# One triangular inverse per level for two directions in an RWKV-7 recurrence, on one Trainium2 core

## The chip, the core and the metric

One Trainium2 chip, one core of it. The metric is the device time of one execution of the whole program, in microseconds, the median of the runs. TensorE (PE in the profile) does the matrix products and reads its moving operand and its weights from SBUF; VectorE (DVE), ScalarE (ACT) and GpSimd (POOL) do the elementwise work; SyncE (SP) issues the DMAs. Everything here is fp32.

## What is computed

Two layers of a hybrid backbone block over 256 context and 512 latent tokens of width 1024. Layer 0 mixes tokens with a bidirectional RWKV-7, layer 1 with grouped-query attention; a SwiGLU feed-forward follows each. The change is in the scan of layer 0, which runs once forward (e = 0) and once backward (e = 1) for each of 16 heads of 64 channels:

```python
def step(S, inp):
    r_t, w_t, k_t, v_t, kk_t, a_t = inp
    sa = jnp.einsum('bhvk,bhk->bhv', S, -kk_t)
    S = (S * w_t[:, :, None, :] + sa[..., None] * (kk_t * a_t)[:, :, None, :]
         + v_t[..., None] * k_t[:, :, None, :])
    return S, jnp.einsum('bhvk,bhk->bhv', S, r_t)
...
for d, rev in enumerate((False, True)):
    S_c, yc_d = rwkv7_scan(S0, r_c, d_c[d], k_c[d], v_c, kk_c, a_c[d], rev)
    _, yl_d = rwkv7_scan(S_c, r_l, d_l[d], k_l[d], v_l, kk_l, a_l[d], rev)
```

## The kernel before

The function `recurrence` (L909) cuts the 768 tokens into 12 chunks of 64 (`CH`) and processes a chunk at a time. Within a chunk the influence of earlier tokens on later ones is a 64x64 triangular system, so for each chunk, head and direction the inverse of a unit triangular matrix is needed. The forward matrix is triangular in one sense, the backward one in the other. Two heads are worked on together (a pair, 8 in all): partitions 0 to 63 hold one head, 64 to 127 the other (`half(h)`). A group is 4 chunks in each direction (`GROUP` = 4), 3 groups a pair, 24 groups in all; each of the tiles `inverse`, `inverse_t`, `lvl` holds 8 matrices of 64 columns, the forward ones in columns 0 to 255, the backward ones in 256 to 511.

The work of a group:

- `score` (PE, L1506 and L1509) and `mask` (DVE, L1778): the score matrices, cut to their triangles, into `sc_b` and `sc_k`.
- The inverse by doubling, in levels n = 0 to 5: at level n the inverse of blocks of 2^n is grown to blocks of 2^(n+1). `cut` (POOL, L2037) multiplies the scores by the mask of the level into `lvl`, 512 columns. `level0` (DVE, L1784) adds the identity. For n = 1 to 5: `t` (PE, L1549) multiplies `lvl` with the transposed inverse so far, 16 products of 64x64; `t_copy` (ACT, L1927) brings them to SBUF as `t_sb`, 512 columns; `y` (PE, L1559 and L1562) multiplies by the inverse so far, 16 products; `add` (DVE, L1790) adds the new blocks, 256 columns; `flip` (DVE, L1799) makes the transpose for the next level. The products of the backward direction have their heads crossed, so `swap` (ACT, L1939) copies the backward half of the inverse with the heads exchanged into `inverse_swapped`, two copies of 64x256 a level.
- The chain over chunks, 4 steps a group, 96 in all: `rhs` (PE, L1620), `rhs_copy` (ACT, L1944), `u` (PE, L1649, with the inverse as weights), `u_copy` (ACT, L1948), `products` (PE, L1664 and others), `update` (DVE, L1809) and `decay` (POOL, L2026).

Beside that run the features of the next pair and the readout of an earlier one (`feature`), on all engines.

The order is written out by hand: `period` is a long list of calls such as `t(at(-5), 3)`, run for each pair, and each engine's class takes from this one list the calls that are its own, in this order. Nothing is reordered afterwards, so an engine whose next instruction waits holds up everything behind it. Two PSUM work areas of two banks (`WORK`) are handed out in turn to `score`, `keys`, `values`, `t`, `y` and side work; `work_free` waits until the previous user of the area has been read.

A product of 64x64 takes a quarter of PE's array: the rows by the half of the partitions that its operands are read from, the columns by the half that its result goes to. In the profile one fp32 product is two MATMUL and two LDWEIGHTS records, so the 16 products of a `t` are 32 MATMUL records.

`values` (PE, L1536) has products in two quarters alone: rows of head h, columns of head 1 - h. The masks are loaded at the start (L1459, L1461).

Of the kernel before, what the change touches and what calls it, by code (L numbers as in the profile page):

```python
# [908 lines left out]
def recurrence(c, d, dram, hidden, full):  # L909

    nc = c.nc
    with ExitStack() as ctx:
# [41 lines left out]
        lvl_ready, t_ready, t_copied, x_ready, x_added, x_turned, x_swapped = (sem(n) for n in (  # L954
            "level_masked", "t_product", "t_copied", "x_products", "x_added", "x_turned", "x_swapped"))
# [13 lines left out]
        by_way = lambda bank: bank[:].rearrange("p (e n) -> p e n", e=2)[:, :, 0:GROUP * CH]  # L969
        def new_columns(units, way, n):  # L970

            size = 1 << n
            return bass.AP(units.tensor, units.offset + size,
                           [units.ap[0], [way - size, 2], [2 * size, GROUP * CH // (2 * size)], [1, size]])

        tokens_of = lambda bank: bank[:, 1024 - TOK:1024]
# [36 lines left out]
        def schedule(E):  # L1013
# [71 lines left out]
            def swap(G, n):  # L1085
                if G:
                    use.take("swap", G.g, n)
                    E.swap(G, n)

# [45 lines left out]
            def period(pair):  # L1135
# [13 lines left out]
                swap(at(-5), 1)  # L1149
# [26 lines left out]
                swap(at(-5), 2)  # L1176
# [16 lines left out]
                swap(at(-5), 3)  # L1193
# [13 lines left out]
                swap(at(-4), 0)  # L1207
# [16 lines left out]
                swap(at(-5), 4)  # L1224
# [9 lines left out]
                swap(at(-4), 1)  # L1234
# [24 lines left out]
                swap(at(-4), 2)  # L1259
# [27 lines left out]
                swap(at(-4), 3)  # L1287
# [5 lines left out]
                swap(at(-3), 0)  # L1293
# [17 lines left out]
                swap(at(-4), 4)  # L1311
# [5 lines left out]
                swap(at(-3), 1)  # L1317
# [25 lines left out]
                swap(at(-3), 2)  # L1343
# [29 lines left out]
                swap(at(-3), 3)  # L1373
# [13 lines left out]
                swap(at(-2), 0)  # L1387
# [19 lines left out]
                swap(at(-3), 4)  # L1407
# [3 lines left out]

            for name in FIRST:
                feature(0, name)
# [12 lines left out]
        with nc.Block() as block:  # L1426
# [338 lines left out]
            def _(dve):  # L1765
                v = nc.vector

                class Dve(Part):

                    def mask(self, G, i):  # L1770
                        dve.wait_ge(scores, self.use.of("score", G.g, i) + 1)
                        need(dve, y_ready, GROUP * (G.g - 3) + 2 * i + 2)
                        if G.g == 0:
                            dve.wait_ge(masks_loaded, 48)
# [1682 lines left out]
```

## Time and profile before

| | us |
|---|---|
| median of 3 runs (2299.14 to 2301.2) | 2301.01 |
| the profiled execution's own time | 2302.0 |
| its span | 2300.2 |
| PE busy | 2042.9 (89%) |
| PE weight loads busy | 1770.0 (77%) |
| DVE busy | 1248.9 (54%) |
| ACT busy | 931.0 (40%) |
| POOL busy | 491.1 (21%) |

The span is from the first to the last instruction of the program; 1.8 us lie around it. A busy share is a union over an engine's records: a MATMUL record of 64 columns lasts some 0.22 us, but the next starts long before it ends, so a busy PE may well be waiting. How fast PE works is read from the starts of its records, not from its busy share. The recurrence's matrices are worked on from about 402 us to 988 us of the span.

### The profile page before, as it was taken

Reading aid. Unit: us, or ns where it says so; the run is one execution under the profiler, and the core shown is the slowest. Engines: PE = TensorE matmul, PEld = TensorE weight load, DVE = VectorE, ACT = ScalarE, POOL = GpSimd, SP = SyncE. Lnnn points to the kernel's source line nnn. Section 1 sums busy time; section 2 is a strip of 40 time slices with the busy share of each in tenths; the row PEclk is TensorE's granted clock in tenths of the full one; section 3 lists DMA queues with packets and bytes.
Section 4 is the critical chain, followed back from the end, with each engine's and each line's share of the span. In section 5 each row is a group of like instructions: output and inputs, shape, how many; then the busy total and the mean of one; then the engine's idle time right before and its main releaser. Section 6 shows DMA issues by size and latency. Waiting matters only on the chain. (4 is left out here: it accounts for less than half of the span.)

```text
span 2300.2 us, 60266 instructions
## 1 busy us (share of the span) xinstructions
PE 2042.9 (89%) x26295; PEld 1770.0 (77%) x26295; DVE 1248.9 (54%) x1816; ACT 931.0 (40%) x1567; POOL 491.1 (21%) x410
## 2 busy tenths in 40 slices
PE   5798997788888887769999999999997988999998
PEld 3597886677767766669999999999863567888887
DVE  4544424677766775332885766755496534333333
ACT  2323324667666664422632322423334533432321
POOL 0011111776667765302000000001220001000000
PEclk8899998999999999979999999999898998999999
DMA  9676764000011000042121212211210012333332
GB/s 315 206 214 199 215 196 132 27 24 20 28 33 34 23 14 12 11 164 63 37 92 58 90 56 74 69 60 39 74 46 19 1 52 67 100 101 91 93 107 84
DMA packets 222295, 192.07 MB, mean 83 GB/s; under 512 B 11482, under 2 KB 206948, under 8 KB 221540
## 3 DMA queue, kind: packets, MB, share of 16 engines
q1 hardware_dynamic: 222052, 188.44, 26.7%
q8 instruction: 199, 3.26, 0.6%
q14 instruction: 44, 0.36, 0.1%
HBM read 170.60 MB, written 17.83 MB: 82 GB/s over the span
## 5 line engine op out<-in xcount | busy, mean ns | idle before, releaser
L2037 POOL TENSOR_TENSOR lvl<-sc_b,level_mask 128x512 f32<-128x512 f32 x144 | 204.6, 1432 | 90.3 <-PE banks L1549 53.6
L530 DVE TENSOR_TENSOR ffn_lo<-ffn_raw,ffn_hi 128x1024 fp32r<-128x1024 f32 (+1 forms) x58 | 77.5, 1335 | 195.3 <-ACT ffn_hi L525 195.3
L550 PE MATMUL banks<-mix_hi,proj_hi 128*128 128x386 f32 (+1 forms) x432 | 152.6, 353 | 14.2 <-DVE proj_lo L530 14.2
L550 PE MATMUL banks<-operand_hi,ffn_w_hi 128*128 128x384 f32 x464 | 156.3, 337 | 4.4 <-DVE operand_lo L496 4.4
L550 PE MATMUL banks<-operand_lo,ffn_w_hi 128*128 128x384 f32 x464 | 156.1, 336 | 0.0
L550 PE MATMUL banks<-operand_hi,ffn_w_lo 128*128 128x384 f32 x464 | 155.9, 336 | 0.0
L420 POOL TENSOR_TENSOR norm_squares<-norm_squares,norm_x 128x768 f32<-128x768 f32 (+1 forms) x18 | 29.8, 1657 | 588.1 <-ACT norm_x L414 588.1
L550 PE MATMUL banks<-mix_lo,proj_hi 128*128 128x386 f32 (+1 forms) x432 | 147.8, 342 | 0.0
L550 PE MATMUL banks<-mix_hi,proj_lo 128*128 128x386 f32 (+1 forms) x432 | 147.6, 342 | 0.0
L550 PE MATMUL banks<-operand_hi,ffn_hi 128*128 128x512 f32 x352 | 138.4, 393 | 5.2 <-DVE operand_lo L496 2.8
L525 ACT CAST ffn_hi<-ffn_raw 128x1024 fp32r<-128x1024 f32 (+1 forms) x60 | 68.3, 1139 | 182.7 <-PE banks L550 182.4
L550 PE MATMUL banks<-operand_hi,ffn_lo 128*128 128x512 f32 x352 | 137.9, 392 | 0.0
L550 PE MATMUL banks<-operand_lo,ffn_hi 128*128 128x512 f32 x352 | 137.9, 392 | 0.0
L2804 ACT CAST ffn_w_hi<-ffn_raw 128x512 fp32r<-128x512 f32 (+1 forms) x116 | 68.8, 605 | 131.7 <-PE banks L550 131.1
L868 POOL TENSOR_TENSOR mix_lo<-mix_full,mix_hi 128x769 fp32r<-128x769 f32 x24 | 40.6, 1692 | 318.0 <-ACT mix_hi L835 318.0
L1549 PE MATMUL banks<-inverse_t,lvl 64*64 64x64 f32 x3840 | 89.6, 225 | 20.4 <-issue 17.2
L550 PE MATMUL banks<-ffn_t_hi,ffn_w_hi 128*128 128x384 f32 x320 | 106.9, 334 | 0.0
L550 PE MATMUL banks<-ffn_t_lo,ffn_w_hi 128*128 128x384 f32 x320 | 106.9, 334 | 0.0
L550 PE MATMUL banks<-ffn_t_hi,ffn_w_lo 128*128 128x384 f32 x320 | 106.9, 334 | 0.0
L550 PEld LDWEIGHTS banks<-mix_hi,proj_hi 128*128 128x128 f32 x432 | 82.6, 191 | 29.7 <-DVE proj_lo L530 14.4
L1939 ACT COPY inverse_swapped<-inverse 64x256 f32<-64x256 f32 x240 | 96.8, 403 | 11.4 <-DVE inverse L1790 6.9
L2971 DVE SCALAR_TENSOR_TENSOR residual_stream<-banks,mod,residual_stream 128x256 f32<-128x256 f32 x144 | 60.8, 477 | 73.4 <-PE banks L550 73.2
(308 smaller groups left out, 6002.0 us busy)
## 6 DMA issues: line engine op xcount, KB each, us to landing
mod_raw<-in_mod_w SPq DMA_DIRECT2D x96, 512.0 KB, 6.1
ffn_raw<-in_ff_w SPq DMA_DIRECT2D x32, 1024.0 KB, 5.3
ffn_raw<-in_ff_w SPq DMA_DIRECT2D x46, 512.0 KB, 3.8
ffn_raw<-in_ff_w SPq DMA_DIRECT2D x16, 704.0 KB, 4.5
proj_raw<-in_rw_wr SPq DMA_DIRECT2D x8, 512.0 KB, 4.5
proj_raw<-in_rw_wk SPq DMA_DIRECT2D x8, 512.0 KB, 4.7
proj_raw<-in_rw_wv SPq DMA_DIRECT2D x8, 512.0 KB, 4.6
rwkv_out_raw<-in_rw_wo SPq DMA_DIRECT2D x8, 512.0 KB, 4.1
```

The lines of the kernel that those rows point to most:

```text
L420: pool.tensor_tensor(self.pool_sum[:, self.at0:], self.pool_sum[:, self.at0:], self.x[:, s, self.at0:], ALU.add)\
L525: signal(act, self.nc.scalar.copy(self.hi[s][:, 0:k_tiles, :], self.raw[s][:, 0:k_tiles, :]), self.rounded, self.at + n + 1)
L530: signal(eng, eng.tensor_tensor(self.lo[s][:, 0:k_tiles, :], self.raw[s][:, 0:k_tiles, :], self.hi[s][:, 0:k_tiles, :].bitcast(F32), ALU.s ...
L550: mm = pe.matmul(out, a, b, start=(first and n == 0), stop=(last and n == 2), skip_group_check=onto)
L868: signal(pool, nc.gpsimd.tensor_tensor(column(mix_lo[q % 2], k), full[s][:], column(mix_hi[q % 2], k).bitcast(F32), ALU.subtract), mix_res ...
L1549: mm = pe.matmul(bank[half(h ^ e), out], lvl[G.parity][n % 2][half(h), w, :], inv_t[G.parity][half(h), w, :], start=True, stop=True)
L1939: ins = a.copy(inv_s[G.parity][half(1 - h)], inv[G.third][half(h), GROUP:2 * GROUP, :])
L2037: g.tensor_tensor(lvl[G.parity][n % 2][:].rearrange("p (e q) t -> p e q t", e=2), sc_b[G.third][:, :, :, 0, :].rearrange("p q e t -> p e q ...
L2804: nc.scalar.copy(w_hi[x.n % SLOTS][:, 0:x.k_tiles, :], source(x)).then_inc(rounded, 1)
L2971: v.scalar_tensor_tensor(h[:, m, at:at + width], c.bank[bank_no(self, "down", part, m, q)][:, col:col + width], c.mod[:, 0, 40 + m, r:r + ...
```

## The change

The forward and the backward correction of a level lie in different blocks of a 64x64 matrix (the one above, the other below the diagonal). The change puts both in one matrix. `t` takes the lower block of one direction and the upper of the other from one `lvl` matrix of 256 columns in all, and reads the inverses of both directions as its moving operand, alternately 2^n columns of one and of the other (`kept_blocks`). `y` likewise (`new_blocks`), and its result lies in PSUM as two runs of columns, as do the scores. `t` and `y` have 8 products each where there were 16, all of them from head h's rows to head h's columns. `t_copy` moves 256 columns where there were 512. `swap`, its tile and its semaphore are gone, from PE's wait too. `cut` has 256 columns for n = 1 to 5, gathered from both directions' scores in runs of 2^n; for n = 0 it is two instructions of 256. The score tiles have another order of dimensions, so that this gathering is one pattern. The masks of both directions are loaded by 8 DMAs where there were 3, the level masks into a tile that is free then (`tok2`), and joined by one POOL instruction over 1536 columns (`join_masks`). The list of calls is the same but for the 15 `swap` calls taken out.

```diff
-        level_mask, score_mask = sb("level_mask", [P, LEVELS, 2, CH]), sb("score_mask", [P, 2, 2, CH])
+        level_mask, score_mask = sb("level_mask", [P, LEVELS, GROUP, CH]), sb("score_mask", [P, 2, 2, 2, CH])
-        sc_b, sc_k = ([sb(f"sc_{n}{s}", [P, GROUP, 2, 2, CH]) for s in range(3)] for n in "bk")
+        sc_b, sc_k = ([sb(f"sc_{n}{s}", [P, 2, 2, GROUP, CH]) for s in range(3)] for n in "bk")
-        inv_s = [sb(f"inverse_swapped{s}", [P, GROUP, CH]) for s in range(2)]
-        t_sb = [sb(f"t_sb{s}", [P, 2 * GROUP, CH]) for s in range(2)]
-        lvl = [[sb(f"lvl{s}{n}", [P, 2 * GROUP, CH]) for n in range(2)] for s in range(2)]
+        t_sb = [sb(f"t_sb{s}", [P, GROUP, CH]) for s in range(2)]
+        lvl = [[sb(f"lvl{s}{n}", [P, (2 - n) * GROUP, CH]) for n in range(2)] for s in range(2)]
...
+        def kept_blocks(units, n, count):
+            size = 1 << n
+            return bass.AP(units.tensor, units.offset, [units.ap[0], [2 * size, count * CH // (2 * size)], [way_units + size, 2], [1, size]])
+        def new_blocks(units, n, count):
+            size = 1 << n
+            return bass.AP(units.tensor, units.offset + size, [units.ap[0], [way_units - size, 2], [2 * size, count * CH // (2 * size)], [1, size]])
+        def lower_blocks(scores, n):
+            size, way = 1 << n, 2 * GROUP * CH
+            return bass.AP(scores.tensor, scores.offset, [scores.ap[0], [2 * size, GROUP * CH // (2 * size)], [way + size, 2], [1, size]])
+        by_way = lambda bank, n: bank[:, 0:GROUP * CH].rearrange("p (b a x) -> p b a x", b=2, x=1 << n)
...
                     def t(self, G, n):
...
                         for q in range(GROUP):
-                            for e in range(2):
-                                w, out = GROUP * e + q, slice(512 * e + q * CH, 512 * e + q * CH + CH)
-                                for h in range(2):
-                                    mm = pe.matmul(bank[half(h ^ e), out], lvl[G.parity][n % 2][half(h), w, :],
-                                                   inv_t[G.parity][half(h), w, :], start=True, stop=True)
+                            for h in range(2):
+                                out = bank[half(h), q * CH:q * CH + CH].rearrange("p (a b x) -> p a b x", b=2, x=1 << n)
+                                mm = pe.matmul(out, lvl[G.parity][n % 2][half(h), q, :],
+                                               kept_blocks(inv_t[G.parity][half(h), q:q + 1, :], n, 1), start=True, stop=True)
...
                     def y(self, G, n):
...
-                        pe.wait_ge(x_swapped, self.use.of("swap", G.g, n - 1) + 1)
                         for q in range(GROUP):
                             for h in range(2):
-                                pe.matmul(bank[half(h), q * CH:q * CH + CH], t_sb[G.parity][half(h), q, :],
-                                          inv[G.third][half(h), q, :], start=True, stop=True)
-                            for h in range(2):
-                                mm = pe.matmul(bank[half(h), 512 + q * CH:512 + q * CH + CH],
-                                               t_sb[G.parity][half(1 - h), GROUP + q, :], inv_s[G.parity][half(1 - h), q, :],
-                                               start=True, stop=True)
+                                out = by_way(bank, n)[half(h), :, q * (CH // 2 >> n):(q + 1) * (CH // 2 >> n), :]
+                                mm = pe.matmul(out, t_sb[G.parity][half(h), q, :],
+                                               new_blocks(inv[G.third][half(h), q:q + 1, :], n, 1), start=True, stop=True)
...
-                        a.copy(t_sb[G.parity][:].rearrange("p (e q) t -> p e (q t)", e=2), by_way(work(self.use, "t", G.g, n)))\
-                            .then_inc(t_copied, 1)
-
-                    def swap(self, G, n):
...
-                        for h in range(2):
-                            ins = a.copy(inv_s[G.parity][half(1 - h)], inv[G.third][half(h), GROUP:2 * GROUP, :])
-                        ins.then_inc(x_swapped, 1)
+                        a.copy(flat(t_sb[G.parity][:]), work(self.use, "t", G.g, n)[:, 0:GROUP * CH]).then_inc(t_copied, 1)
...
+                    def join_masks(self):
+                        pool.wait_ge(masks_loaded, 128)
+                        ways = [tok[2][:, e, 0:LEVELS, :].unsqueeze(2).to_broadcast([P, LEVELS, GROUP, CH]) for e in range(2)]
+                        g.tensor_tensor(level_mask[:], ways[0], ways[1], ALU.add).then_inc(masks_joined, 1)
...
-                        g.tensor_tensor(lvl[G.parity][n % 2][:].rearrange("p (e q) t -> p e q t", e=2),
-                                        sc_b[G.third][:, :, :, 0, :].rearrange("p q e t -> p e q t"),
-                                        level_mask[:, n].unsqueeze(2).to_broadcast([P, 2, GROUP, CH]), ALU.mult)\
-                            .then_inc(lvl_ready, 1)
+                        if n == 0:
+                            for e in range(2):
+                                ins = g.tensor_tensor(lvl[G.parity][0][:, e * GROUP:(e + 1) * GROUP], sc_b[G.third][:, 1 - e, 0],
+                                                      level_mask[:, 0], ALU.mult)
+                        else:
+                            blocks = {"b": 2, "x": 1 << n}
+                            ins = g.tensor_tensor(flat(lvl[G.parity][n % 2][:, 0:GROUP]).rearrange("p (a b x) -> p a b x", **blocks),
+                                                  lower_blocks(sc_b[G.third][:], n),
+                                                  flat(level_mask[:, n]).rearrange("p (a b x) -> p a b x", **blocks), ALU.mult)
+                        ins.then_inc(lvl_ready, 1)
```

In the order of ACT's instructions, a stretch of the steady part of the recurrence before (copies `tok`, `t_sb`, `inverse_swapped`, `rhs`, `u_sb` and the side work of the features):

```order
401 L1948 COPY u_sb<-banks 128x128
402 L1915 COPY tok<-banks 128x1024
403 L1927 COPY t_sb<-banks 128x512
404 L1939 COPY inverse_swapped<-inverse 64x256 x2
405 L1927 COPY t_sb<-banks 128x512
406 L1944 COPY rhs<-banks 128x128
407 L1975 ACTIVATE ep<-cum 128x12x64
408 L1948 COPY u_sb<-banks 128x128
```

and the same place of another pair in the changed kernel (its lines have other numbers):

```order
415 L1907 COPY tok<-banks 128x1024
416 L1919 COPY t_sb<-banks 128x256 x2
417 L1923 COPY rhs<-banks 128x128
418 L1954 ACTIVATE ep<-cum 128x12x64
419 L1927 COPY u_sb<-banks 128x128
```

The copies of the swapped inverse are gone, those of `t_sb` have half the columns, and all else stands in its old order. On PE, near the recurrence's start, before:

```order
1470 L1549 MATMUL banks<-inverse_t,lvl 64x64 x32
1471 L1559 MATMUL banks<-inverse,t_sb 64x64 x2
1472 L1562 MATMUL banks<-inverse_swapped,t_sb 64x64 x2
...
1487 L1536 MATMUL banks<-centre_heads,v_pair 64x64 x16
1488 L1549 MATMUL banks<-inverse_t,lvl 64x64 x32
```

and now:

```order
1449 L1544 MATMUL banks<-inverse_t,lvl 64x64 x16
1450 L1554 MATMUL banks<-inverse,t_sb 64x2x32 x16
1451 L1532 MATMUL banks<-centre_heads,v_pair 64x64 x16
1452 L1544 MATMUL banks<-inverse_t,lvl 64x64 x16
```

Two `t` and two `y` one behind the other have 16 products each where they had 32, and the `values` products stand where they stood.

## Rows read from the trace of the kernel before

**Rows 1.** Busy time by stretch of the recurrence; the x is the number of records
```profile
core 0: us, PE busy (x) PEld busy (x) DVE busy (x) ACT busy (x) POOL busy (x), PEclk, DMA share, GB/s
480.00:900.00 420.00, 345.20 (x13087) 295.11 (x13088) 289.27 (x434) 269.34 (x545) 289.55 (x259) 0.98 0.09 26
sum 586.00, PE 474.64 PEld 404.34 DVE 375.88 ACT 356.89 POOL 376.91; mean PE 158.21 PEld 134.78 DVE 125.29 ACT 118.96 POOL 125.64
```
**Rows 2.** PE's waits from 402 to 988 us: total us, times, longest us
```profile
PE banks L1549 <- issue: 17.2, 17, 2.2
PE banks L1562 <- issue: 7.7, 8, 1.3
...
PE banks L1559 <- issue: 6.8, 8, 1.2
PE banks L1620 <- DVE state L1809: 6.0, 7, 1.3
PE banks L1664 <- ACT u_sb L1948: 5.7, 15, 0.5
...
PE banks L1689 <- issue: 0.6, 1, 0.6
```
**Rows 3.** Instruction queue, 402 to 988, then 480 to 900 us: packets, MB, share
```profile
q8 instruction: 141, 2.31, 1.6%
...
q8 instruction: 104, 1.70, 1.7%
```
**Rows 4.** PE in order of time: start us, us, what, records, idle before
```profile
502.76 0.27 PE L1593 MATMUL banks<-vtok,tok 64*64 64x64 f32 x2 [1.22 <-issue]
502.89 0.27 PE L1559 MATMUL banks<-inverse,t_sb 64*64 64x64 f32 x2
...
503.38 0.31 PE L1506 MATMUL banks<-ar,b 64*64 64x128 f32 x2
...
556.21 0.63 PE L1536 MATMUL banks<-centre_heads,v_pair 64*64 64x64 f32 x15
556.71 0.27 PE L1559 MATMUL banks<-inverse,t_sb 64*64 64x64 f32 x2
```
**Rows 5.** Groups by line and shape, ACT and POOL: busy us, mean ns, idle before
```profile
L1939 ACT COPY inverse_swapped<-inverse 64x256 f32<-64x256 f32 x240 | 96.8, 403 | 11.4 <-DVE inverse L1790 6.9
L1927 ACT COPY t_sb<-banks 128x512 f32<-128x512 f32 x120 | 70.1, 585 | 55.1 <-PE banks L1549 55.1
L1921 ACT COPY vtok<-banks 128x256 f32<-128x256 f32 x8 | 3.0, 373 | 7.2 <-PE banks L1536 7.2
L2037 POOL TENSOR_TENSOR lvl<-sc_b,level_mask 128x512 f32<-128x512 f32 x144 | 204.6, 1432 | 90.3 <-PE banks L1549 53.6 <-DVE sc_b L1778 31.7 <-DVE inverse L1784 5.0
L2015 POOL TENSOR_TENSOR diag<-ident_heads,ends 128x256 f32<-128x256 f32 x44 | 26.9, 630 | 0.0
```
**Rows 6.** POOL, then DVE, in order of time at the recurrence's start
```profile
386.53 3.04 POOL L2015 TENSOR_TENSOR diag<-ident_heads,ends 128x256 f32<-128x256 f32 x4 [27.48 <-DVE ends L1874]
403.38 2.48 POOL L2037 TENSOR_TENSOR lvl<-sc_b,level_mask 128x512 f32<-128x512 f32 x2 [13.81 <-DVE sc_b L1778]
...
397.70 0.69 DVE L1778 TENSOR_TENSOR sc_b<-banks,score_mask 128x512 f32<-128x512 f32 x1 [1.24 <-PE banks L1509]
```
**Rows 7.** SP's DMA issues at the start, and the level masks' time to landing
```profile
375.16 1.29 SPq L1461 DMA_DIRECT2D level_mask<-in_k_level_mask  x2
376.49 1.44 SPq L1463 DMA_DIRECT2D lora_w<-in_rw_w  x1
...
DMA to landing us min/median/max: 5.5/5.9/6.2
```
**Rows 8.** Stretches of 3.4 us, columns as in Rows 1
```profile
719.70:723.10 3.40, 2.66 (x52) 2.58 (x55) 1.96 (x3) 1.22 (x2) 1.05 (x3) 1.00 0.20 63
723.10:726.50 3.40, 3.40 (x134) 3.40 (x132) 1.91 (x4) 1.75 (x5) 2.06 (x2) 0.51 0.26 77
...
791.40:794.80 3.40, 2.47 (x57) 2.26 (x49) 3.00 (x6) 2.02 (x3) 0.92 (x3) 1.00 0.23 63
794.80:798.20 3.40, 3.40 (x95) 3.38 (x99) 0.51 (x2) 1.83 (x5) 0.86 (x1) 0.50 0.23 58
...
941.60:945.00 3.40, 1.45 (x92) 1.31 (x84) 2.08 (x3) 1.18 (x2) 2.98 (x4) 1.00 0.02 5
945.00:948.40 3.40, 3.07 (x80) 2.76 (x73) 1.03 (x3) 1.66 (x4) 1.63 (x2) 0.50 0.02 5
```

More of the change, by code:

```diff
@@ L1083, in flip @@
                     E.flip(G, n)
[L1085 to L1088, printed above, removed]
             def following(G, q):
@@ L1410, in period @@
                 diag(at(-1))
+            E.join_masks()
             for name in FIRST:
@@ L1422, in recurrence @@
             score = mask = keys = keys_copy = values = values_copy = diag = cut = level0 = nothing
-            t = t_copy = y = add = flip = swap = early = feature = nothing
+            t = t_copy = y = add = flip = early = feature = join_masks = nothing
             rhs = rhs_copy = u = u_copy = products = decay = update = nothing
@@ L1458, in _ @@
                 sp.dma_start(v_s[0][:], dram[2][:, 0, :]).then_inc(slices[0], 16)
-                sp.dma_start(score_mask[:], d["k_score_mask"][:, :, 0:2, :]).then_inc(masks_loaded, 16)
                 for h in range(2):
-                    sp.dma_start(level_mask[half(h)], d["k_level_mask"][half(h)][:, :, :, half(h)]).then_inc(masks_loaded, 16)
+                    for e in range(2):
+                        sp.dma_start(tok[2][half(h), e, 0:LEVELS, :], d["k_level_mask"][half(h)][:, :, e, half(h)]).then_inc(masks_loaded, 16)
+                for e in range(2):
+                    for q in range(2):
+                        sp.dma_start(score_mask[:, 1 - e, :, q, :], d["k_score_mask"][:, e, 0:2, :]).then_inc(masks_loaded, 16)
                 for n, w in enumerate(("rw_w2", "rw_a2")):
@@ L1586, in rhs_values @@
                         for h in range(2):
-                            pe.matmul(CHAIN[G.step(q) % 2][half(h), e * CH:e * CH + CH], sc_k[G.third][half(1 - h), q, e, 0, :],
+                            pe.matmul(CHAIN[G.step(q) % 2][half(h), e * CH:e * CH + CH], sc_k[G.third][half(1 - h), 1 - e, 0, q, :],
                                       vtok[G.pair][half(1 - h), n, :], start=(e == 0), stop=False, skip_group_check=True)
@@ L1603, in y_values @@
                         for h in range(2):
-                            mm = pe.matmul(y[half(h), out], vtok[G.pair][half(1 - h), n, :], sc_k[G.third][half(1 - h), q, e, 1, :],
+                            mm = pe.matmul(y[half(h), out], vtok[G.pair][half(1 - h), n, :], sc_k[G.third][half(1 - h), 1 - e, 1, q, :],
                                            start=opens, stop=False, skip_group_check=True)
@@ L1671, in products @@
                                 mm = pe.matmul(Y_BANK[n // 8][half(h), n % 8 * CH:n % 8 * CH + CH], u_sb[half(h), e, :],
-                                               sc_b[G.third][half(h), q, e, 1, :], start=False, stop=True, skip_group_check=True)
+                                               sc_b[G.third][half(h), 1 - e, 1, q, :], start=False, stop=True, skip_group_check=True)
                             if e == 1:
@@ L1788, in add @@
                         dve.wait_ge(x_ready, self.use.of("y", G.g, n) + 1)
-                        x = new_columns(inv[G.third][:], GROUP * CH, n)
-                        v.tensor_tensor(x, new_columns(work(self.use, "y", G.g, n), 512, n), x, ALU.add).then_inc(x_added, 1)
+                        x = new_blocks(inv[G.third][:], n, GROUP)
+                        v.tensor_tensor(x, by_way(work(self.use, "y", G.g, n), n), x, ALU.add).then_inc(x_added, 1)
                     def flip(self, G, n):
@@ L2036, in cut @@
                             pool.wait_ge(t_ready, self.use.of("t", G.g, n - 2) + 1)
[L2037 to L2040 removed]
+                        if G.g == 0:
+                            pool.wait_ge(masks_joined, 1)
+                        if n == 0:
+                            for e in range(2):
+                                ins = g.tensor_tensor(lvl[G.parity][0][:, e * GROUP:(e + 1) * GROUP], sc_b[G.third][:, 1 - e, 0],
[6 more added lines that the diff above has]
+                        ins.then_inc(lvl_ready, 1)
                     def feature(self, t, name):
```

49 lines of the change are left out of this document (14 added, 35 removed).

## The prediction

> **What bounds the kernel now.** I read busy time by stretch first, then PE's waits, then the DMA queue of instructions, then single stretches in order of time.
>
> Busy time by stretch: from 402 to 988 us the recurrence has the core to itself. PE is busy 475 of 586 us, DVE 376, ACT 357, POOL 377 [rows 1]. So PE is the busiest by far, but a record of 64 columns counts 0.22 us busy while its successors start far sooner, and the question is what holds the starts up.
>
> PE's waits answer it. In 18 rows of the form "<- issue", of which the first two, one more and the last stand in [rows 2], PE sat idle 82 us in 79 pauses of about 1.0 us, the longest 2.2 us. In such a pause PE waits for nothing that the profile shows. For all other engines together it waited 25.5 us (15 rows, the two largest in [rows 2]). As a pause is counted from the end of a 0.22 us record whose successor would have started 0.06 us after it, each is some 0.16 us longer: 82 + 79 x 0.16 = 95 us. So of PE's 586 us about 95 go to pauses without a releaser, 25 to 40 to other engines, and the rest is its own work at its own pace.
>
> What the pauses are: the instruction queue made 141 transfers in this stretch [rows 3]. From 480 to 900 us there are 13087 matmul and 13088 load records [rows 1], in which the queue made 104 transfers [rows 3]: 252 records a transfer. No other engine of the core has instructions in such numbers. In order of time a pause of 1.22 us stands in the middle of a row of products that had all their data [rows 4]. I read this as PE using up instructions faster than they arrive: a transfer comes every 586 / 141 = 4.2 us, and where the products are quick, PE gets to the end of what it has.
>
> How quick they are: a `y` of 32 matmul records began at 502.89, and the next work at 503.38, so it takes 0.49 us [rows 4]. With as many loads that is 64 records in 0.49 us, or one transfer's worth in 1.9 us, less than half the 4.2 us. The half as many records of `values`, which run in two quarters of the array alone, took from 556.21 to 556.71, 0.50 us [rows 4].
>
> The Trainium skill, page "Runtime: NRT & Kernel Launch", section "Instruction fetch mechanics", says that instructions come in blocks of 256 and that crossing a block is "mostly hidden". The block agrees with the 252 records here; the "mostly hidden" does not agree with 79 pauses. By that page the pauses would be something else, which is a rival below.
>
> **The change, part by part.** The sum is made against the profiled execution, 2302.0 us, and then carried to the median of the runs, 2301.0.
>
> *Pace of `t` and `y`.* The products are halved, 240 blocks of 16 become 240 of 8, but the 8 lie in two quarters only, like `values`. So a block takes 0.50 us where it took 0.49 [rows 4]: 240 x 0.01 = +2 us. Bounds: +5 us, and -10 us where a neighbour in another quarter starts earlier. The halving of the products in itself buys nothing.
>
> *Supply of instructions.* It removes 3840 matmul records and as many loads, 7680 / 252 = 30 transfers of 141. At the mean price of a transfer, 82 / 141 = 0.58 us, that is -18 us, the lower bound of the gain. But the records that go are those that were used up fastest, and the 240 blocks that stay use a transfer's worth in 252 / 32 x 0.50 = 3.9 us instead of 1.9, about as slowly as transfers come. At most all pauses go, -95 us. I take -60: the pauses in `t` and `y` themselves (17.2 + 7.7 + 6.8 us in 33 pauses [rows 2], with 0.16 each 37 us) and somewhat under half of the other 58.
>
> *ACT.* 240 copies of `inverse_swapped` go, 96.8 us of ACT's time, and 120 copies of `t_sb` shrink to the width of the first copy of `vtok`, 373 ns for 585: another 25 us [rows 5]. Nearly all of it lies beside PE's work and is hidden. What comes to the path is PE's waiting for ACT, 11.6 us in all (7 rows, 5.7 us of it for `u_sb` [rows 2]), behind which a swap copy often stood. I take half, -6 us; bounds 0 and -12.
>
> *POOL.* Of 144 `cut` instructions at 1432 ns, 120 have half the width; a `diag` of 256 columns takes 630 ns [rows 5]: some 95 us of POOL's time. The other 24 become two each of 630, no gain. Hidden work again: PE waits for POOL directly in no row. DVE gets its instructions through a little sooner where both use SBUF. 0, with the ACT term's bounds. Gathering in runs of 2^n may make `cut` slower than 630 ns; even at 1432 it would stand where it stands.
>
> *What is late next.* The pauses gave the others time. Without 60 us of them DVE is busy 376 of some 545 us (69% for 64%), still far from full, but the order is fixed and PE meets its inputs earlier: the `state` from DVE (6.0 us now [rows 2]), the scores after `mask`, the transposed inverse after `flip`. Bounds: 0, and +50 us, which would be twice the 25.5 that PE waits for others now. I take +20.
>
> *Clock.* After sparse stretches PE's granted clock falls from 1.00 to 0.50 or 0.51, that is from 2.4 to 1.2 GHz, for a while: after 52, 57 and 92 records in 3.4 us [rows 8]. In the steady part it is 0.98 on the mean [rows 1], about 17 of 420 us at the low level. With fewer records and half the array in use in `t` and `y`, this will be more frequent. A stretch of 3.4 us at half clock loses at most 1.7 us of streaming. I take 5 to 8 more of them, +8 us; bounds 0 and the rival below.
>
> *The start.* Five more DMA issues at 0.65 us (two took 1.29 [rows 7]) delay what is queued on SP behind them, the weights of pair 1 first, by 3.2 us. The masks land 5.9 us after their issue [rows 7], by 388 us; `join_masks` has 1536 columns, 3.7 us at the 1.24 us that `cut` takes for 512 (2.48 us for two [rows 6]). The three microseconds of `diag` then end by 395 us, and POOL waited until 403.38 for the scores [rows 6]. `mask` waits at 397.70 for PE, not for the loads. The cover is 8 us of POOL's idling; without it the cost would be 3.7 us once. 0.
>
> Sum: +2 - 60 - 6 + 20 + 8 = -36 us, so 2266 for the profiled execution and **2265 us** for the median.
>
> **The rivals.** A measurement of this kernel can tell some 0.2%, 4.6 us, from no change.
>
> *A. Supply was everything.* The slower pace ends nearly all pauses (-95), and the lighter ACT and POOL keep up, so that only +10 comes back: +2 - 95 - 6 + 10 + 8 = -81, 2220 us. For it: even outside `t` and `y` the pauses come with quick blocks, and 22% fewer transfers spread over the time gives 548 / 111 = 4.9 us between them. Against it: score, key and chain products stay as quick as they are.
>
> *B. Only the share of the removed records.* The remaining 111 transfers keep their 0.58 us: -18 - 6 + 8 + 2 = -14, 2287 us.
>
> *C. The clock falls, and it is slower.* Place: PE from 420 to 950 us. The steady part has 13087 / 420 x 3.4 = 106 matmul records in 3.4 us [rows 1]; without 3840 of some 17800 over 548 us there are 87, so that stretches as sparse as those before the falls of [rows 8] become more frequent. Each further stretch at half clock costs up to 1.7 us, some 1.1 where waits absorb a part. It decides from 26 to 40 further stretches on (44 us over 1.7 or 1.1); at 60 of them, +66 for the +8, the time is 2323 us. Against it: records with 128 columns or the whole array stay, and the idle pauses, which made stretches sparse, get fewer.
>
> *D. The pauses are not supply.* Then they stay, and what is left is -6 from ACT, +2 from pace and a few us for the clock: 2297 to 2302, no change. This is what the page of the Trainium skill named above would make of it.
>
> *E. Gathered operands stream slowly, and it is slower.* The moving operand of `t` and `y` is now read in runs of 2^n elements, at level 1 two elements of one direction and two of the other. No row of before has such a product, so the price is bounded from 0 to a second 0.49 us for each of 240 blocks. If every level paid, +118 - 36 = +82, 2383 us; if level 1 alone (48 blocks), +24, and it stays faster. The Trainium skill, page "Advanced Engine Details and Errata", section "Memory Cachelines", says that a line of SBUF is 16 bytes and wants two hits, and that PSUM patterns that are not contiguous slow matmuls significantly; level 1 has just two hits, and the results of `y` and of the scores are two long runs each in PSUM. By its first rule E would not occur, by the second it might. The trace of before shows neither.
>
> **How the numbers follow.** The forecast (2250 to 2281) gets 0.50, since it takes the middle of a term whose two ends are A and B; A 0.20; B 0.13; C 0.07; D 0.06; E 0.04. Faster by over 0.2% are the first three, 0.83; within 0.2% is D, 0.06; slower are C and E, 0.11. The likeliest case is the forecast, 2265 us. The range reaches down past A's 2220 to 2212 and up past B to the beginning of D, 2297; beyond it lie C, E, half of D and a little below A, under 0.2.
>
> **What would show it.** Right: 109 to 113 transfers on the instruction queue in the recurrence where there were 141, PE's "issue" rows at 20 to 40 us for 82, a `t` or `y` block still 0.48 to 0.52 us from its start to the next work, `t_sb` copies at 370 to 380 ns, `cut` at 620 to 750 ns, PE's waits for DVE, ACT and POOL at 40 to 50 us for 25.5. Wrong: pauses as many and as long as before (D); `t` blocks of level 1 clearly longer than those of level 5 (E); a mean granted clock under 0.9 in the steady part (C); or the pauses gone and PE waiting on DVE for as long, in which case the order is what bounds it and the term "what is late next" was too small.

## The result, and the profile after

| | before | the change |
|---|---|---|
| median of the runs, side by side | 2300.07 us (2296.75 to 2301.2, 4 runs) | 2229.9 us (2227.58 to 2234.77, 4 runs) |
| ratio | | 0.9698, 95% interval [0.9681, 0.9716] |
| the profiled execution's own time, its span | 2302.0, 2300.2 | 2227.58, 2225.7 |
| ACT busy | 931.0 | 811.9 |
| POOL busy | 491.1 | 431.3 |
| last `u_sb` copy, the end of the recurrence | 986.5 | 911.9 |

The change is 70 us faster, in the profiled pair 74.5. All of it lies in the recurrence: what follows the last `u_sb` copy takes as long as before, and at the first of its 96 steps nothing is gained yet (-2.5 us). Then the gain grows evenly: 19 us after 36 steps, 39 after 60, 63 after 84.

Busy time by stretch, the last stretch ending with the recurrence; answers to [rows 1]:

```profile
core 0: us, PE busy (x) PEld busy (x) DVE busy (x) ACT busy (x) POOL busy (x), PEclk, DMA share, GB/s
402.00:480.00 78.00, 68.66 (x1686) 54.61 (x1682) 51.10 (x76) 36.03 (x62) 48.45 (x51) 0.88 0.07 20
480.00:830.00 350.00, 315.95 (x9825) 272.73 (x9824) 259.20 (x411) 179.11 (x361) 236.34 (x266) 1.00 0.10 28
830.00:914.00 84.00, 70.67 (x2468) 62.87 (x2464) 44.02 (x86) 24.85 (x75) 28.93 (x47) 1.00 0.04 13
sum 512.00, PE 455.29 PEld 390.21 DVE 354.33 ACT 240.00 POOL 313.72; mean PE 151.76 PEld 130.07 DVE 118.11 ACT 80.00 POOL 104.57
```

ACT has lost a third of its work and POOL a sixth, while PE's busy time fell by only 19 us (475 to 455), as its 8 products take about as long as 16 did. The steady part runs at full clock.

PE's waits from 402 to 914 us, the queue of instructions, and the changed groups of ACT and POOL; answers to [rows 2], [rows 3] and [rows 5]:

```profile
PE banks L1611 <- DVE state L1799: 8.4, 10, 1.3
PE banks L1655 <- ACT u_sb L1927: 6.2, 15, 0.5
PE banks L1544 <- issue: 6.1, 9, 1.3
PE banks L1554 <- issue: 5.0, 6, 1.4
PE banks L1517 <- issue: 3.8, 4, 1.1
PE banks L1502 <- DVE sc_k L1768: 3.4, 6, 1.0
```
```profile
q8 instruction: 111, 1.82, 1.5%
```
```profile
L1919 ACT COPY t_sb<-banks 128x256 f32<-128x256 f32 x120 | 44.9, 374 | 68.2 <-PE banks L1544 68.1
...
L2030 POOL TENSOR_TENSOR lvl<-sc_b,level_mask 128x256 f32<-128x256 f32 x120 | 102.6, 860 | 55.3 <-PE banks L1544 48.9 <-DVE inverse L1774 5.0 <-DVE tmp L1831 1.3
...
L2026 POOL TENSOR_TENSOR lvl<-sc_b,level_mask 128x256 f32<-128x256 f32 x48 | 37.6, 804 | 33.6 <-DVE sc_b L1768 33.6
```

The rows "<- issue" sum to 27.1 us in 38 pauses, where there were 82.3 in 79. All waits for other engines together are 24.9 us, where there were 25.5: PE comes 70 us sooner, and finds its inputs as ready as before. The queue made 111 transfers for 141.

PE in order of time, two `t` of level 4 (L1544, moving operand in runs of 16) at 506.50 and 552.64, two of level 1 (runs of 2) at 511.15 and 554.11, the last with a `y` (L1554) behind it:

```profile
506.50 0.68 PE L1544 MATMUL banks<-inverse_t,lvl 64*64 64x64 f32 x16
507.11 0.44 PE L1680 MATMUL banks<-ident,norm_y 128*64 128x128 f32 x4
...
511.15 0.66 PE L1544 MATMUL banks<-inverse_t,lvl 64*64 64x64 f32 x16
511.68 0.39 PE L1655 MATMUL banks<-u_sb,tok 64*64 64x64 f32 x6
...
552.64 0.66 PE L1544 MATMUL banks<-inverse_t,lvl 64*64 64x64 f32 x16
553.19 0.39 PE L1655 MATMUL banks<-u_sb,tok 64*64 64x64 f32 x6
...
554.11 0.70 PE L1544 MATMUL banks<-inverse_t,lvl 64*64 64x64 f32 x16 [0.23 <-ACT tok L1907]
554.64 0.63 PE L1554 MATMUL banks<-inverse,t_sb 64*64 64x64 f32 x16
555.11 0.34 PE L1611 MATMUL banks<-state,ar 64*64 64x64 f32 x6
```

From its start to the next work a `t` of level 1 takes 0.53 us both times, one of level 4 0.55 and 0.61, a `y` 0.47. With half the products a block takes what the block of 16 took [rows 4]. Over all blocks that ran on without a pause, from the first to the last record's start, the medians are 478 ns for `t` of level 1 and 415 to 463 ns for the other levels, so short runs cost 15 to 60 ns in 48 blocks (24 of `t`, 24 of `y`), 3 us at most.

### The profile page after: what moved, and what is told of

It is laid out like the page before. It is cut to its first block and busy times, and to the rows that moved or that the text cites. A ratio compares the mean times of both kernels' runs of the same rounds, so it can differ in the third digit from the quotient of the medians.

```text
span 2225.7 us, 52361 instructions
## 1 busy us (share of the span) xinstructions
PE 2024.8 (91%) x22455; PEld 1756.4 (79%) x22455; DVE 1230.2 (55%) x1816; ACT 811.9 (36%) x1327; POOL 431.3 (19%) x435
## 5 line engine op out<-in xcount | busy, mean ns | idle before, releaser
L2030 POOL TENSOR_TENSOR lvl<-sc_b,level_mask 128x256 f32<-128x256 f32 x120 | 102.6, 860 | 55.3 <-PE banks L1544 48.9
L1544 PE MATMUL banks<-inverse_t,lvl 64*64 64x64 f32 x1920 | 82.3, 223 | 11.0 <-issue 6.1
L2868 DVE TENSOR_TENSOR ffn_w_lo<-ffn_raw,ffn_w_hi 128x512 fp32r<-128x512 f32 (+1 forms) x112 | 77.5, 693 | 26.8 <-ACT ffn_w_hi L2797 25.2
```

What stands on the lines that cost most here:

```text
L1544: mm = pe.matmul(out, lvl[G.parity][n % 2][half(h), q, :], kept_blocks(inv_t[G.parity][half(h), q:q + 1, :], n, 1), start=True, stop=True)
L2030: ins = g.tensor_tensor(flat(lvl[G.parity][n % 2][:, 0:GROUP]).rearrange("p (a b x) -> p a b x", **blocks), lower_blocks(sc_b[G.third][:], n),
L2868: v.tensor_tensor(w_lo[x.n % SLOTS][:, k, :], source(x), w_hi[x.n % SLOTS][:, k, :].bitcast(F32), ALU.subtract)\
```

## The experiments

Four theories were to be told apart. **Supply**: PE uses up instructions faster than they arrive, and fewer of them is what helps. **Load**: the lighter ACT and POOL (and the shorter waits behind them) are what helps. **Array**: PE gains because there is less to multiply. **Pace**: what is left of the recurrence is PE's own speed in the two quarters. The first four kernels ran on one chip (before there 2310.88 us), the other four on one again (before 2309.27 us). The interval stands behind each ratio to before; the recurrence ends with the start of the last `u_sb` copy. "Start to start" stands for this split of a profiled recurrence: of the distances between the starts of successive MATMUL records, those over 0.75 us that no other engine ended are the long pauses, the others with an idle PE in them are the waits, and all the rest is PE's own time.

| kernel | median us | ratio to before | transfers | issue pauses | recurrence ends |
|---|---|---|---|---|---|
| ACT's part alone | 2311.46 | 1.0012 [0.9989, 1.0035] | 141 | 94.0 us, 80 | 997.3 |
| ACT's and POOL's parts | 2313.68 | 1.0014 [0.9992, 1.0035] | 141 | 94.5, 85 | 998.4 |
| 8 products, all else as before | 2234.67 | 0.9673 [0.9648, 0.9697] | 111 | 21.0, 37 | 921.2 |
| the change, padded to 16 | 2316.07 | 1.0029 [1.0006, 1.0051] | 142 | 92.1, 85 | 1007.4 |
| the change again | 2233.92 | 0.9689 [0.9646, 0.9732] | 111 | 25.3, 36 | 920.5 |
| the change, `y` padded | 2270.26 | 0.9840 [0.9796, 0.9884] | 126 | 58.2, 56 | 956.1 |
| the change, four quarters | 2216.46 | 0.9609 [0.9568, 0.9650] | 112 | 38.8, 43 | 903.4 |
| the change, whole array in `y` | 2283.57 | 0.9897 [0.9873, 0.9922] | 104 | 3.6, 7 | 966.6 |

**ACT's part alone**, in the kernel before: no `swap`, `t_copy` of 256 columns; PE keeps its 16 products.

```diff
-                        pe.wait_ge(x_swapped, self.use.of("swap", G.g, n - 1) + 1)
...
-                                               t_sb[G.parity][half(1 - h), GROUP + q, :], inv_s[G.parity][half(1 - h), q, :],
+                                               t_sb[G.parity][half(1 - h), q, :], inv[G.third][half(1 - h), GROUP + q, :],
...
-                        a.copy(t_sb[G.parity][:].rearrange("p (e q) t -> p e (q t)", e=2), by_way(work(self.use, "t", G.g, n)))\
+                        a.copy(flat(t_sb[G.parity][:, 0:GROUP]), work(self.use, "t", G.g, n)[:, 0:GROUP * CH]).then_inc(t_copied, 1)
```

> The kernel before with ACT's part of the change alone: the copies of the swapped inverse are left out and t_sb is copied at 256 columns; PE keeps all its 16 products a block (the backward ones read unswapped operands, so the inverse of the backward direction is not computed). Supply theory (the gain is the pauses of PE between instruction blocks): 141 transfers and some 80 us of issue pauses stay, the time falls by 5 to 15 us from before, to about 2290. Load theory (the gain is the lighter ACT and POOL): most of the 70 us appears here, 2250 or less.

**ACT's and POOL's parts**: the same, and `cut` of 256 columns for n = 1 to 5.

```diff
+                            g.tensor_tensor(lvl[G.parity][n % 2][:, 0:GROUP], sc_b[G.third][:, :, 0, 0, :],
+                                            level_mask[:, n, 0].unsqueeze(1).to_broadcast([P, GROUP, CH]), ALU.mult)\
+                                .then_inc(lvl_ready, 1)
```

> As e1_act_alone, and POOL's cut at 256 columns for levels 1 to 5 as well (what it leaves out is the backward half). Supply theory: within 5 us of e1_act_alone, about 2287, pauses unchanged. Load theory: 2240 or less, the whole gain but what the products give.

Neither moved the time, with 118 us of ACT's work and 70 of POOL's gone; the 5 to 15 us that I had expected from ACT even by the supply theory did not come. In the second kernel from 480 to 900 us, and PE's first waits:

```profile
480.00:900.00 420.00, 341.28 (x12860) 291.62 (x12849) 268.62 (x423) 185.29 (x371) 237.88 (x254) 0.98 0.09 24
```
```profile
PE banks L1549 <- issue: 21.2, 18, 2.5
PE banks L1561 <- issue: 9.6, 7, 2.4
PE banks L1558 <- issue: 7.2, 8, 1.9
```

ACT is busy 185 us there instead of 269 [rows 1], and the pauses are all there. They are even 12 us more than in the profile of before, but that was taken on another chip, where the kernel before was some 10 us quicker; there is no trace of before from this one. The load theory falls.

**8 products, all else as before**: the forward products alone, with `swap`, both `t_sb` halves and the wide `cut` kept.

```diff
-                            for e in range(2):
+                            for e in range(1):
...
-                            for h in range(2):
-                                mm = pe.matmul(bank[half(h), 512 + q * CH:512 + q * CH + CH],
-                                               t_sb[G.parity][half(1 - h), GROUP + q, :], inv_s[G.parity][half(1 - h), q, :],
-                                               start=True, stop=True)
```

> The kernel before with the forward products alone in t and y, 8 a block in two quarters of the array; every copy, cut, swap, add and wait of before stays at its full width (left out: the backward direction's correction). Supply theory: about 111 transfers, issue pauses 25 to 40 us, and 50 to 65 us less than before, about 2240. Load theory: ACT and POOL are as loaded as before, so 2285 or more.

The whole gain is there with none of ACT's and POOL's relief (ACT is busy 355 us of 520, PE 467; in the change, run again below, 242 and 463). The pauses fell further than the 25 us expected at the least, to 21.0:

```profile
480.00:830.00 350.00, 321.52 (x9723) 274.71 (x9720) 273.06 (x407) 257.01 (x520) 281.83 (x242) 0.98 0.10 28
```

**The change, padded to 16**: 8 further products behind the 8 of each `t` and `y`, in the quarters that stand idle, into PSUM columns that nobody reads.

```diff
+                            for h in range(2):
+                                mm = pe.matmul(bank[half(1 - h), 512 + q * CH:512 + q * CH + CH], lvl[G.parity][n % 2][half(h), q, :],
+                                               inv_t[G.parity][half(h), q, :], start=True, stop=True)
```

> The changed kernel with each block of t and y brought back to 16 products: 8 more, in the two quarters of the array that stand free, into PSUM columns that nobody reads. Supply theory: as the extra ones run beside the others, a block keeps its 0.46 to 0.50 us, but transfers return to 141 and pauses to some 80 us, and the time rises by 50 to 65 us over the changed kernel, to about 2285. Load theory: ACT and POOL are as light as in the changed kernel, so within 10 us of its 2230.

All of the gain is given back and 5 to 7 us more, with ACT and POOL as light as in the change; I had expected 50 to 65 us over the change, and it was 82 to 86. Start to start against the change run again, the long pauses rose by 82 us (33 to 116), PE's own time by 11 and the waits fell by 8; PE had the lower granted clock (0.50, that is 1.2 GHz) for 71 us of the recurrence there and for 37 in the change, which may be those 11. This also settles the array theory in one direction: products in idle quarters cost little in the array (median from the first to the last record's start 466 ns for 463 in `t`, 464 for 415 in `y`, 6 us in all), and yet some 80 us of time.

**The change again, and with `y` alone padded**, half of the dose.

> The change itself once more, beside the next three kernels, so that they can be set against it under the same conditions. Every theory: ratio to the kernel before 0.968 to 0.972, 109 to 113 transfers on the instruction queue from 402 us to the end of the recurrence, issue pauses of 25 to 30 us.

> The change, with 8 further products beside the 8 of each y (in the two quarters of the array that stood idle; their results go to PSUM columns that nobody reads) and t left at 8. Half the dose of the padding: 1920 more MATMUL records and as many loads, 15 transfers more than the change, 126. Theory supply: the time rises with the dose, issue pauses 50 to 65 us in 50 to 60, ratio to before 0.982 to 0.988, that is 30 to 45 us above the change. Theory array (the products of y and t are themselves what takes the time, whatever the number of instructions): no difference to the change, since the blocks take 0.5 us either way. A third, that only the first of the removed products mattered (some threshold above which the pauses are there in full): ratio 0.999 to 1.003.

PE's longest wait in the second of them, and its queue of instructions:

```profile
PE banks L1544 <- issue: 11.0, 8, 2.1
```
```profile
q8 instruction: 126, 2.06, 1.6%
```

The time follows the number of transfers: 111, 126 and 142 give 2234, 2270 and 2316 us (the last on the other chip, where before was 2 us slower), some 2.3 to 2.9 us a transfer, and the pauses 25, 58 and 92 us. Between these three there is no threshold. From 111 to 126, start to start, the long pauses rose by 38 us, the waits fell by 3, and PE's own time did not change. The pauses in `t` (L1544), which was not touched here, went from 5.8 to 11.0 us: the instructions that `y` uses up are missing elsewhere.

**Where the pauses stand.** The number of instructions could act in another way than through their transfer, so I set the pauses beside the transfers of 16 KB themselves, packet by packet in the traces. In all ten kernels together, 396 of the 397 issue pauses over 0.6 us end 1.15 to 1.70 us after the last transfer has landed (median 1.4 us), where a moment taken at random falls into that window in 10 to 13% of cases. Before, the distances from one such pause to the next are 64; all lie within 12 records of a multiple of 252, and 40 of them at 250 to 254. So the pauses stand at the edges of the transferred blocks and end with the arrival of the next. Before, 40 pairs of them are one block apart, and there the time from the end of one pause to the end of the next has a median of 3.9 us: some 1.35 until the next transfer starts, 1.05 for the transfer, 1.4 until PE goes on. Where PE uses up block after block in less than that, it ends up waiting.

**The change in four quarters**: every second chunk's products go to the other half of the columns, and with it to another PSUM bank (the two were not taken apart).

```diff
-                                out = bank[half(h), q * CH:q * CH + CH].rearrange("p (a b x) -> p a b x", b=2, x=1 << n)
+                                side = bank[:, 512 * (q % 2):512 * (q % 2) + GROUP * CH]
+                                out = side[half((h + q) % 2), q * CH:q * CH + CH].rearrange("p (a b x) -> p a b x", b=2, x=1 << n)
```

> The change, with the products of every second chunk of t and y going to the other half of the array's columns (and another PSUM bank), so that the 8 products lie in four quarters. Left out: the inverse is held at zero (add and level0 multiply where they added), so the output is not the reference's. The number of instructions is that of the change, 111 transfers. A block should take 0.25 to 0.30 us where it takes 0.45. Theory pace (what is left is PE's own speed in the array): 240 blocks x 0.2 us = 48 us less than the change, ratio to before 0.947 to 0.952. Theory supply: PE reaches the end of its instructions sooner and waits there: issue pauses rise from 27 to 45 to 70 us, the time falls by 0 to 20 us against the change, ratio 0.961 to 0.970.

PE in order of time, a `y` (L1556) and the work behind it, then a `t` (L1545), and its waits:

```profile
541.48 0.46 PE L1556 MATMUL banks<-inverse,t_sb 64*64 64x64 f32 x16
541.77 0.22 PE L1642 MATMUL banks<-rhs,inverse 64*64 64x64 f32 x2
...
552.14 0.46 PE L1545 MATMUL banks<-inverse_t,lvl 64*64 64x64 f32 x16
552.51 0.45 PE L1657 MATMUL banks<-u_sb,tok 64*64 64x64 f32 x8
```
```profile
PE banks L1556 <- issue: 7.2, 7, 1.3
PE banks L1545 <- issue: 7.0, 9, 1.3
```

A block takes 0.29 and 0.37 us here; over all that ran on without a pause, the median from the first record's start to the last is 242 ns for `t`, where it was 463, and 231 for `y`, where it was 415, so 240 blocks are quicker by some 0.2 us, 50 us in all. The time fell by 17.5. Part of the 50 us never reached PE's sequence: what stands behind a block starts later after its last record (150 ns for 106 behind `t`, 135 for 52 behind `y`), and start to start PE's own time fell by 37 us. The long pauses rose by 16 (33 to 49) and the waits by 4, which leaves 17. The issue rows, 38.8 us, stayed under the 45 to 70 expected by the supply theory. So PE's own speed is now a part of what bounds the recurrence, and supply takes back a good part of what is saved there. With the inverse kept, every second chunk's matrices of one head would have to lie in the other head's half of the partitions, which is what `swap` paid for; that was not tried.

**The whole array in `y`**: one product of 128 rows and 128 columns for both heads of a chunk, with a block-diagonal `t_sb`.

```diff
-                                mm = pe.matmul(out, t_sb[G.parity][half(h), q, :],
-                                               new_blocks(inv[G.third][half(h), q:q + 1, :], n, 1), start=True, stop=True)
+                            mm = pe.matmul(out, t_sb[G.parity][:, q].rearrange("p h t -> p (h t)"),
+                                           new_blocks(inv[G.third][:, q:q + 1, :], n, 1), start=True, stop=True)
...
-                        a.copy(flat(t_sb[G.parity][:]), work(self.use, "t", G.g, n)[:, 0:GROUP * CH]).then_inc(t_copied, 1)
+                        for h in range(2):
+                            ins = a.copy(t_sb[G.parity][half(h), :, h, :],
+                                         work(self.use, "t", G.g, n)[half(h), 0:GROUP * CH].rearrange("p (q t) -> p q t", t=CH))
+                        ins.then_inc(t_copied, 1)
```

> The change, with both heads' products of a chunk in y made one product of the whole array (128 rows, 128 columns of weights): t_sb holds a block-diagonal matrix whose other blocks are set to zero once at the start, 4 products for 8, the same result. It removes 960 MATMUL records and as many loads more, 103 or 104 transfers. ACT pays: t_copy is two copies of 64x256 at some 0.40 us each for one of 0.37, so 120 x 0.43 = 52 us more of ACT's time, and each level's t_sb comes 0.4 us later. Theory supply: 7.6 transfers fewer, a gain between their share of the remaining pauses (7.6 / 111 x 39 = 3 us) and 2 us each (15 us), less what of the later t_sb comes to the path (0 to 10): 12 us under the change to 5 above it; I take 5 under, ratio to before 0.966 to 0.969. Theory load (ACT's work counts): slower than the change by 10 to 50 us, PE's waits for t_sb at 10 us or more.

It was meant as a better version and is 50 us slower than the change. I expected 5 us faster. The groups of `y`, of `t_copy`, and PE in order of time:

```profile
L1553 PE MATMUL banks<-inverse,t_sb 128*128 128x64 f32 x960 | 137.4, 288 | 1.0 <-ACT t_sb L1919 0.9
L1553 PEld LDWEIGHTS banks<-inverse,t_sb 128*128 128x128 f32 x960 | 120.9, 198 | 15.3 <-ACT t_sb L1919 4.7 <-issue 3.1
...
L1919 ACT COPY t_sb<-banks 64x256 f32<-64x256 f32 x240 | 88.0, 366 | 57.8 <-PE banks L1544 55.9
```
```profile
563.90 1.10 PE L1553 MATMUL banks<-inverse,t_sb 128*128 128x64 f32 x8
564.93 0.39 PE L1610 MATMUL banks<-state,ar 64*64 64x64 f32 x6
```

The supply half came out as the theory has it and better: 3.6 us of issue pauses are left, in 7. The waits for `t_sb` are 0.9 us, so ACT's doubled copies cost next to nothing, against the load theory once more. But a block of 8 records takes 1.03 us where 16 took 0.47: 120 x 0.56 = +67 us of pace, less 22 us of pauses, 45, and the recurrence ends 46 us later. Start to start it is +80 for PE's own time, -23 for the long pauses and -11 for the waits. The figure that I had left out is the price of products of the whole array. Two parts of it stand in the trace. Within a block the MATMUL records start 0.11 us apart, with a load's start half-way between two of them, so that loads and products take turns; in the quarters each quarter starts a record every 0.06 us. And going over from quarters to the whole array and back costs too: 148 ns before the first record and 205 behind the last (medians), where it was 51 and 52, some 0.25 us of the 0.64 that a block lost. I read the first part as the price of loading weights 128 columns wide with no other quarter at work beside it; no run varies the loads alone, so this is not shown. The Trainium skill, page "TensorEngine Tiling (Array Packing)", section "Key Properties", says that tiles load weights and multiply in parallel, independently. The four-quarter blocks agree with it (231 and 242 ns for 415 and 463), and in these blocks, of one tile, loads and products take turns.

## Why the prediction was right, and where it was not

The direction, the range and the mechanism held. The number was off by half: -36 us forecast, -70 measured, nearer to rival A's 2220 than to the forecast's 2265. That is luck for A, whose -95 us of pauses did not come; its sum is near because it gave less back. The forecast had the supply term right and lost half of it again by two terms of the wrong size or sign, +20 and +8. For each term, in the profiled pair, start to start:

| term | forecast | measured |
|---|---|---|
| supply of instructions | -60 | long pauses: 97.3 us in 71 to 34.2 us in 31, **-63** |
| what is late next | +20 | waits and shorter pauses 43.5 to 42.8, **-1**; waits for other engines by the rows 25.5 to 24.9 |
| clock, and pace of `t` and `y` | +8, +2 | PE's own time 443 to 433, **-10** together |
| ACT | -6 | 0 by the first experiment; the change's waits for ACT are 8.3 us for 11.6 |
| POOL | 0 | 0 by the second experiment |
| the start | 0 | 0 gained at step 0; 2.5 us later there, within what kernels with the old masks show among themselves (436.8 to 444.0 us) |
| sum | -36 | -74 |

*Supply.* "At most all pauses go ... I take -60" was right, and for the reason given: the quick records go, and the 240 blocks that stay use instructions up as slowly as they come. The lower bound, the mean price of a transfer (0.58 us), was far from it. A transfer's worth less is worth 2.3 us or more in these runs, since a pause is the difference of two larger times, the 3.9 us from block to block and what PE needs to use one up. Rival B, which took the mean, falls with it. Rival D falls too: the pauses answer to the number of instructions (padding) and to how fast they are used up (four quarters), not to the load of ACT and POOL, and they end with the arrival of a block. The Trainium skill, page "Runtime: NRT & Kernel Launch", section "Instruction fetch mechanics", has the crossing of a block of 256 as "mostly hidden". The block agrees with 252 records a transfer; "hidden" does not agree with 92 us of pauses at 142 transfers and 3.6 at 104.

*What is late next.* This is the step that failed. "PE meets its inputs earlier" is true, but I priced it by what PE waited before, as if the others could not move. They moved too. ACT and DVE spend most of their idle time waiting for PE: in the change ACT idled 68 us for L1544 alone before its `t_sb` copies. When PE comes sooner, so do they. I take it that what PE finds is decided by the distance between the calls in the list, in instructions and not in microseconds; no run moved a call to test this. With a recurrence 17 us shorter still (four quarters) the waits for other engines were 29.3 us, against 26.9 in the change beside it. The term should have been 0 to +5.

*Clock.* "With fewer records and half the array in use ... this will be more frequent" was wrong in sign. Before, the last stretch of the recurrence ran at 0.89:

```profile
900.00:988.00 88.00, 65.22 (x2517) 57.96 (x2516) 32.32 (x65) 35.62 (x94) 29.40 (x36) 0.89 0.03 8
```

By the trace's own records of the granted clock PE spent 39 us of the recurrence at 0.50, that is 1.2 GHz, before (7 of them before 480 us), and 22 us after, of which 19 in one piece at the start, to 420.6 us. I had counted records per time, which fall from 106 to 95 in 3.4 us (I had 87); but the stretches in front of a fall before [rows 8] each hold an issue pause of 0.9 to 2.0 us, and it is the pauses that went. 17 us less at half clock are worth up to 8 us; the profiles don't separate that from the blocks' own pace. Rival C falls: the change's mean clock is 1.00 from 480 us to the recurrence's end.

*Pace.* "A block takes 0.50 us where it took 0.49" held within a few hundredths: from the first to the last record's start the median was 476 ns before and is 415 to 478 by line and level. `y`, whose results lie in PSUM in two runs, is no slower than `t`: 442 ns against 463 over all levels. Rival E falls: level 1 costs 60 ns a block at most and not 490. The Trainium skill, page "Advanced Engine Details and Errata", section "Memory Cachelines", lets runs of two elements pass without loss. The trace agrees, to within these 60 ns in 450.

*Expected rows.* Right: 111 transfers (109 to 113), issue rows of 27.1 us (20 to 40), `t_sb` copies of 374 ns (370 to 380), block times. Wrong: the waits for other engines, 24.9 us (40 to 50), and `cut`, 860 ns on the mean for 620 to 750. Its level-0 form, which gathers nothing, takes 804, and the medians of all levels lie at 726 to 745, so the gathering is not the reason. The longer `cut` cost nothing that shows: in the second experiment 70 us of POOL's work made no difference.

## What to carry to other kernels

Where PE works through many small products, count its instructions and the transfers of the instruction queue, and look for waits "<- issue" of about a microsecond; if they are there, an instruction less is worth more than its share, even one that runs in an idle quarter of the array and would cost nothing by its duration. Set against this what the merged product costs: packing two directions into one 64x64 product kept the pace, packing two heads into one 128x128 product removed the pauses and lost three times as much in PE's pace. And don't charge a faster engine with waits for the others when those are idle because they wait for it.

## What the runs showed of the hardware

- A block of instructions of 16 KB held some 252 MATMUL and LDWEIGHTS records. Where PE ran out of them, it went on 1.4 us after the next block had landed (median; 396 of 397 long issue pauses 1.15 to 1.70 us after), and block followed block in 3.9 us (median of 40 pairs before; 3.9 to 4.1 in the five other kernels with 16 or more such pairs).
- The highest rate at which PE's instructions went over a long stretch is much the same in the three kernels with 80 pauses: from 480 to 900 us, MATMUL and LDWEIGHTS records together, 26175 / 420 = 62 a us before [rows 1], 25709 / 420 = 61 with ACT's and POOL's parts, and 61 in the padded kernel, whose blocks are others. The change goes at 19649 / 350 = 56, and still has 34 us of long pauses.
- 8 products in two quarters take 0.47 to 0.61 us from their start to the next work, 16 in four quarters 0.49 [rows 4], 8 in four quarters 0.29 and 0.37, and 4 in the whole array 1.03. From the first to the last record's start, the medians of a `t` are 463, 476 and 242 ns for the first three.
- Moving operands in alternating runs of two fp32 elements from two places 256 columns apart cost at most 60 ns in a block of 8 products.
